# A two-layer encoder on one core: the last chunk's first tile goes between the halves of the second tile's gate and up product

## The reference

```
x = x + 0.5 * swiglu(rms_norm(x, ffn1_norm), gate, up, down)       # "first FFN" of the layer
h = rms_norm(x, mix_norm); proj = h @ w_in                         # mixer: convolution module and
y = g0 * conv_module(proj) + g1 * attention(proj); x = x + y @ w_out   # attention, gated and merged
x = x + 0.5 * swiglu(rms_norm(x, ffn2_norm), gate, up, down)       # "second FFN"
swiglu(h) = (silu(h @ w_gate) * (h @ w_up)) @ w_down               # 1024 -> 2816 -> 1024
```

## Time and profile before

| | us |
|---|---|
| median of three runs | 1025.88 (1025.52 to 1025.89) |
| the profiled execution | 1025.66 |
| its span in the trace | 1023.9 |
| PE busy | 1018.2 (99%) |
| DVE busy | 846.4 (83%) |
| ACT busy | 660.8 (65%) |
| POOL busy | 330.8 (32%) |

### The profile page before, as it was taken

The page is one execution under the profiler, slowest core; times in us unless marked ns, Lnnn a source line. Parts: engine busy times, 40 slices in busy tenths (PEclk is TensorE's granted clock), DMA queues, the critical chain, the costliest instruction groups (busy, mean ns, idle before and its releaser), DMA issues.

```text
span 1023.9 us, 13331 instructions
## 1 busy us (share of the span) xinstructions
PE 1018.2 (99%) x4905; PEld 853.9 (83%) x4905; DVE 846.4 (83%) x1008; ACT 660.8 (65%) x836; POOL 330.8 (32%) x258
## 2 busy tenths in 40 slices
PE   9999999999999999999999999999999999999998
PEld 6888888998888888888888888889988888888887
DVE  6999977698976898888679889866999678988972
ACT  6767665576874575766557666647778556666761
POOL 2999400138850100000049990001589300000000
PEclk9999999999999999999999999999999999999999
DMA  8968578555544596748749574975366365947491
GB/s 278 309 191 277 162 209 274 160 185 176 207 161 128 182 328 183 244 140 234 228 154 339 166 226 135 274 248 174 127 214 226 123 173 185 331 140 233 158 240 42
DMA packets 175185, 208.99 MB, mean 204 GB/s; under 512 B 64112, under 2 KB 129936, under 8 KB 175120
## 3 DMA queue, kind: packets, MB, share of 16 engines
q1 hardware_dynamic: 173904, 206.03, 64.9%
q10 hardware_dynamic: 1216, 2.11, 0.7%
HBM read 192.90 MB, written 1.05 MB: 189 GB/s over the span
## 4 chain that ended last, share of the span: by engine, by line
PE 98%; ACT 1%; DVE 1%; DMA 0%; issue 0%; POOL 0%; ACTq 0%
PE bank L829 30%; PE bank L831 30%; PE bank L830 30%; PE bank L966 1%; PE bank L1128 1%; PE bank L1137 1%; PE bank L1158 1%; PE bank L868 0%; PE bank L1136 0%; PE bank L1160 0%; PE bank L836 0%; DMA cacc<-in_ffn_norm 0%; DVE htok L1902 0%; DVE x L1950 0%; ACT htok L1357 0%; PE bank L1146 0%
## 5 line engine op out<-in xcount | busy, mean ns | idle before, releaser
L1854 DVE TENSOR_TENSOR wlo<-raw,whi 128x2048 fp32r<-128x2048 f32 (+2 forms) x136 | 308.9, 2283 | 21.0 <-ACT whi L1344 21.0
L1344 ACT ACTIVATE whi<-raw 128x2048 fp32r<-128x2048 f32 (+2 forms) x160 | 302.9, 1910 | 25.3 <-DMA raw<-in_ffn_w_down 16.5
L829 PE MATMUL bank<-whi,hThi 128*128 128x512 f32 (+1 forms) x816 | 316.1, 387 | 0.0
L831 PE MATMUL bank<-whi,hTlo 128*128 128x512 f32 (+1 forms) x816 | 311.4, 382 | 0.0
L830 PE MATMUL bank<-wlo,hThi 128*128 128x512 f32 (+1 forms) x816 | 311.3, 381 | 0.0
L697 POOL TENSOR_TENSOR small<-small,expo 128x1 f32<-128x1 f32 (+3 forms) x20 | 30.0, 1505 | 470.5 <-DVE small L1895 432.9
L831 PEld LDWEIGHTS bank<-whi,hTlo 128*128 128x128 f32 x816 | 153.2, 188 | 29.6
L829 PEld LDWEIGHTS bank<-whi,hThi 128*128 128x128 f32 x816 | 153.3, 188 | 28.8
L830 PEld LDWEIGHTS bank<-wlo,hThi 128*128 128x128 f32 x816 | 153.4, 188 | 28.4
L829 PE MATMUL bank<-whi,gThi 128*128 128x512 f32 (+1 forms) x416 | 162.3, 390 | 0.0
L831 PE MATMUL bank<-whi,gTlo 128*128 128x512 f32 (+1 forms) x416 | 161.2, 388 | 0.0
(11 more groups left out here) (201 smaller groups left out, 1359.0 us busy)
## 6 DMA issues: line engine op xcount, KB each, us to landing
raw<-in_ffn_w_down SPq DMA_DIRECT2D x88, 512.0 KB, 4.7
raw<-in_ffn_w_gate SPq DMA_DIRECT2D x68, 512.0 KB, 4.2
raw<-in_ffn_w_up SPq DMA_DIRECT2D x68, 512.0 KB, 5.2
raw<-in_w_in SPq DMA_DIRECT2D x48, 512.0 KB, 4.9
htok<-in_ffn_w_gate SPq DMA_DIRECT2D x16, 512.0 KB, 6.1
heads<-in_ffn_w_up SPq DMA_DIRECT2D x16, 512.0 KB, 6.8
raw<-in_w_out SPq DMA_DIRECT2D x16, 512.0 KB, 4.6
raw<-in_w_in SPq DMA_DIRECT2D x8, 544.0 KB, 5.2
```

The lines of the kernel that those rows point to most:

```text
L829: nc.tensor.matmul(out, lh, rh, start=start, stop=False, skip_group_check=skip)
L831: return nc.tensor.matmul(out, ll, rh, start=False, stop=stop, skip_group_check=skip)
L1344: nc.scalar.activation(whi[:, slot(u, RING), 0:USED[u]], src, ACT.Copy).then_inc(whi_ready, 1)
L1854: nc.vector.tensor_tensor(wlo[:, slot(u, RING), 0:n], src, whi[:, slot(u, RING), 0:n].bitcast(F32), ALU.subtract).then_inc(wlo_ready, 1)
```

## The change

PE's program of the last chunk is put in another order. Its instructions are the same, and no other engine's program is touched. Where PE did everything of tile 0 and then everything of tile 1, it now does gate_up(10, 0), down(8, 0), the first half of gate_up(10, 1), then turn(10, 0), down(9, 0) and down(10, 0), then the second half of gate_up(10, 1), and the rest of tile 1 as before. This applies to all four FFNs.

```diff
                 def last():
                     c = NCH - 1
-                    for t in range(TT):
-                        gate_up(c, t)
-                        down(c - 2, t)
-                        turn(c, t)
-                        down(c - 1, t)
-                        down(c, t, last=True)
+                    def first_tile():
+                        turn(c, 0)
+                        down(c - 1, 0)
+                        down(c, 0, last=True)
+
+                    gate_up(c, 0)
+                    down(c - 2, 0)
+                    gate_up(c, 1, between=first_tile)
+                    down(c - 2, 1)
+                    turn(c, 1)
+                    down(c - 1, 1)
+                    down(c, 1, last=True)
```

## The result

The changed kernel takes 1033.29 us (1033.16 to 1033.55, four runs) against 1025.89 us (1025.52 to 1026.31): a ratio of 1.007, interval 1.0058 to 1.0082, 7.4 us slower where 6.2 us were forecast. The profiled execution took 1033.37 us for a span of 1031.5. In a second set of runs (the first experiment) the same kernel was 6.0 us slower, so one pair of medians places the loss only within about 1.5 us; part of what follows is on why.

The account below looks back on a forecast made before the run. PE was taken to bound the kernel. Two first FFNs at 2.1 us, layer 0's second FFN at 2.0 and the last at 0 made 6.2 us, giving a forecast of 1032.0 us, range 1028.9 to 1034.1.

Parts of the forecast that it names:

- The bound and the zero on the gain side: PE sets the time and nearly never waits, so earlier unit release and longer cover gain 0 on PE.
- the longer cover: 12 more matmuls between down(8, 0) and turn(10, 0); worth 0, since PE shows no wait at either turn.
- The earlier release of the unit: First half of gate_up(10, 1) frees a weight unit earlier, ending ACT's 0.37 us wait; worth 0 on PE.
- Residual of tile 0 later by 2.72 us: turn(10, 0), down(9, 0), down(10, 0) and so the residual come 12 matmuls later, 2.72 us.
- First FFNs: In each layer PE waits 1.33 us at turn(10, 1), inside a 2.1 us total delay at tile 1's transposes.
- Second FFN of layer 0: PE waits 2.0 us at down(10, 1) for rest_gu, bounds 0.9 to 2.2 us; 0 to 0.1 us at the turn.
- the second join: On DVE in layer 0's second FFN, ahead of rest_gu: waits for a later transposing DMA, about 2.6 us later.
- Last FFN: DVE idled 4.72 us between residual and mul; 2.0 us of that are left, so 0 us.
- The sum: Over all four FFNs, 2 x 2.1 + 2.0 + 0 = 6.2 us slower.
- The clock: Third rival, chance 0.03: clock falls to 1.2 GHz behind three waits, 8.2 us more, 14.4 us in all, 1040.3.

Follow-up runs that it names:

- turn_early: Changed kernel with turn(10, 0) and down(9, 0) back in their old places, only down(10, 0) moved: 1031.97 us against 1025.30 for the kernel before.
- silu_first: Changed kernel with silu(10, 1) on ACT and mul(10, 1) on DVE moved up in the first FFNs: 1032.83 us against 1025.30 for the kernel before.
- again: The changed kernel run once more, unaltered: 1031.73 us against 1025.77 for the kernel before.
- only_second0: Kernel before with the new order in the second FFN of layer 0 alone: 1028.48 us against 1025.77.
- only_last: Kernel before with the new order in the last FFN alone: 1025.22 us against 1025.77.
- only_first: Kernel before with the new order in the two first FFNs alone: 1029.61 us against 1025.77.
- dose3: Changed kernel with the first tile's work after 3 instead of 12 matmuls of gate_up(10, 1): 1025.91 us against 1026.02 for the kernel before.
- dose6: Changed kernel with the first tile's work after 6 instead of 12 matmuls of gate_up(10, 1): 1027.77 us against 1025.30 for the kernel before.
- rest_first: Changed kernel with rest_gu(10, 1) ahead of DVE's weight remainder in layer 0's second FFN: 1030.86 us against 1026.02 for the kernel before.
- dose24: Changed kernel with the first tile's work behind all 24 matmuls of gate_up(10, 1) instead of 12: 1041.62 us against 1025.30 for the kernel before.

## Why the prediction was right

**The bound and the zero on the gain side.** PE had no wait to be shortened, and none was: in turn_early, with the turn of tile 0 in its old place and so without the longer cover, the loss is the same to 0.1 us. The earlier release of the unit did end ACT's wait of 0.37 us, as forecast, but ACT then waited 0.27 us for norm_apply; it was not tested alone.

**Residual of tile 0 later by 2.72 us.** Measured 2.76 in the change, less the opening.

**First FFNs.** 1.33 us at the turn: 1.38 and 1.32 measured. 2.1 us at the transposes by a late residual of tile 1, with the turn's wait inside it: 2.13 and 2.07. No wait at down(10, 1): none. That the loss is set by the last of these waits, whatever the one at the turn is, is shown by silu_first.

**Second FFN of layer 0.** 2.0 us through the second join: 2.05 to 2.16 in the four traces with this wait and the clock at 1.00 (the change, again, only_second0, turn_early). Both joins waited for their DMA, and rest_gu ended at 517.26, which less the 3.04 us by which this trace was late at the turn is 514.2, where 514.3 was forecast. No wait at the turn: none.

**Last FFN.** 0: 0.0.

**The sum.** 6.2 us was 6.35 in the change's trace and 6.2 in its second. The medians moved by 7.4 and 6.0 us. What the prediction left out is the scatter outside the FFN ends: the opening varies by over 1.5 us between executions, mainly by when the clock rises in the warming matmuls, and the profiled execution of before sat about in the middle of that; layer 1's mixer varies by some 0.7 us (0.17 us shorter to 0.57 us longer than in the trace of before). That 1032.0 lies between the two measured medians is in part luck: it added 6.2 us to an opening in mid-range.

**The clock.** I gave the rival 0.03 and priced it as 8.2 us for all three places. In the change's two profiled executions the clock stayed at 1.00 behind the waits. But two of its first four executions and one of four in the second set had a mean clock of 0.998 over the span, the mean that silu_first's trace has with its one fall. Over all sets 7 of the 24 executions with the whole wait of the second FFN of layer 0 had 0.998 (the change, again, only_second0, turn_early, silu_first). None of the 38 of only_last, only_first, dose3, dose6 and rest_first had less than 0.999, and none of the 44 of before in the experiments' sets; for those of its first set the clock isn't on record. In only_second0, with the new order at this place alone, it was two of eight, and in only_first and rest_first, with both waits at turns, none of eight. (dose24, with its longer waits, had 0.995 to 0.997.) So it is a matter of one place in some executions; my rival had it at all three or nowhere. That is inferred from the counts, since only silu_first's execution has a trace. What a fall costs is known from that trace, 1.6 us at the marks, and doesn't stand out in the other times: the change's two executions at 0.998 took 1033.21 and 1033.16 us, the two at 1.000 1033.37 and 1033.55.

## What to carry to other kernels

Where one engine is full and its program is reordered, the order alone may cost nothing (only_last: none); look for the semaphore that comes later and read on the other engines what stands between it and the next thing the full engine needs, in queue order. The slack of that chain, here 0.6 us, can be read before the change from idle times and ends, and beyond it each microsecond of delay was a microsecond of time. Waits along one chain can't be added up as separate prices; the last one counts. When a difference of under 1% is to be explained, split both traces at marks along the span first, so that an opening that scatters by a microsecond isn't explained as part of the change.

## What the runs showed of the hardware

The granted clock fell to its lower level behind all three waits at turns in dose24, of 3.9 us in the first FFNs and of 2.55 us in the second FFN of layer 0, and behind a wait of 1.78 us in silu_first; four other traces, with waits of 1.72 to 1.78 us at that same place, kept 1.00. The wait of 2.55 us and the stretch behind it in dose24:

```profile
517.25 0.44 PE L1028 MATMUL bank<-ident,gates 128*128 128x128 f32 x2 [2.55 <-DVE gates L1970]
```

```profile
517.50:520.00 2.50, 2.50 (x9) 2.03 (x8) 1.90 (x3) 2.50 (x7) 0.00 (x0) 0.59 0.30 56
```

So a wait of the same length at the same place may or may not cost the clock. When it fell, six to eight matmuls of 512 columns ran 0.43 us apart.

The ten warming matmuls of the opening ran for 2.32 to 4.07 us in different executions, most single ones being 0.38 or 0.63 us in the records, and the whole kernel shifts with them: the clock's full level was first on record between 4.48 us (only_last) and 8.57 us (the change), against 6.74 us in before, and the openings of these two were 0.89 us earlier and 0.89 us later than before's. Two traces are off that order, only_second0 (5.41 us) and silu_first (4.67 us), with openings only 0.07 and 0.34 us early; PE waits 0.5 and 0.6 us for ACT's rounded weights at line 966 in both and in no other. The Trainium skill, "TensorE: Matmul & The Clock Gate", section "Part 1: The HAM clock gate", says that where the clock rises varies from run to run; the traces agree, with the three times above.
